# RWKV-7 scan: b and k transposed by VectorE blocks and ScalarE copies in place of TensorE

## The reference, cut to what matters

```python
def _rwkv7_scan(r, decay, k, v, kk, a, reverse):
    def step(S, inp):
        r_t, w_t, k_t, v_t, kk_t, a_t = inp
        sa = jnp.einsum('bhij,bhj->bhi', S, -kk_t)
        S = (S * w_t[:, :, None, :] + sa[..., None] * (kk_t * a_t)[:, :, None, :]
             + v_t[..., None] * k_t[:, :, None, :])
        y = jnp.einsum('bhij,bhj->bhi', S, r_t)
        return S, y
```

## Time and profile before

| | |
|---|---|
| median of 3 runs | 3921.93 us (3916.46 to 3925.49) |
| the profiled execution: its own time | 3919.46 us |
| its span, first to last instruction | 3917.7 us |
| mean granted TensorE clock | 0.964 of full |
| TensorE matmul busy, whole program | 3565.0 us, 91% |
| VectorE busy | 1859.1 us, 47% |
| ScalarE busy | 908.8 us, 23% |
| GpSimd busy | 179.5 us, 5% |
| the scan phase | from about 1660 to 2131 us of the span |

### The profile page before, as it was taken

How to read it: one execution, slowest core, us unless ns; L and a number is a source line. 1 busy time by engine, 2 the same in 40 slices (tenths; PEclk the granted TensorE clock), 3 DMA queues, 4 the chain that set the end, 5 groups by cost and what they waited for, 6 DMA issues and landing times. The chain is left out here.

```text
span 3917.7 us, 68126 instructions
## 1 busy us (share of the span) xinstructions
PE 3565.0 (91%) x28504; PEld 3035.6 (77%) x28504; DVE 1859.1 (47%) x2745; ACT 908.8 (23%) x1332; POOL 179.5 (5%) x336
## 2 busy tenths in 40 slices
PE   6999999999799991989998899777969999999997
PEld 5888888887677880989987677667858888888885
DVE  4544544544566206756655343303164544544546
ACT  2111111110433214433333622213031111111112
POOL 0000000000000000522221000000000000000000
PEclk9999999999899995999999999889989999999999
DMA  3010010010236312033333330110010110100101
GB/s 114 32 48 32 32 48 32 32 37 11 95 92 155 122 67 85 1 116 86 85 84 117 105 132 16 33 44 22 22 43 33 43 37 32 46 34 32 48 6 54
DMA packets 86028, 225.75 MB, mean 58 GB/s; under 512 B 6736, under 2 KB 53456, under 8 KB 79824
## 3 DMA queue, kind: packets, MB, share of 16 engines
q1 hardware_dynamic: 81808, 210.91, 16.9%
q10 hardware_dynamic: 4032, 12.06, 0.8%
HBM read 176.07 MB, written 46.87 MB: 57 GB/s over the span
## 5 line engine op out<-in xcount | busy, mean ns | idle before, releaser
L298 DVE TENSOR_TENSOR main_acc<-main_acc,ffn_psum 128x512 f32<-128x512 f32 (+1 forms) x1056 | 617.3, 598 | 853.8 <-PE ffn_psum L221 853.1
L210 PE MATMUL ffn_psum<-x_xh,ffn_wi_h 128*128 128x512 f32 (+1 forms) x2112 | 525.5, 357 | 49.3 <-DVE ffn_wi_l L287 49.3
L210 PE MATMUL ffn_psum<-x_xl,ffn_wi_h 128*128 128x512 f32 (+1 forms) x2112 | 525.3, 357 | 0.0
L210 PE MATMUL ffn_psum<-x_xh,ffn_wi_l 128*128 128x512 f32 (+1 forms) x2112 | 525.1, 357 | 0.0
L210 PEld LDWEIGHTS ffn_psum<-x_xh,ffn_wi_h 128*128 128x128 f32 x2112 | 372.8, 188 | 117.4 <-DVE ffn_wi_l L287 49.7
L210 PEld LDWEIGHTS ffn_psum<-x_xl,ffn_wi_h 128*128 128x128 f32 x2112 | 349.6, 188 | 61.3
L210 PEld LDWEIGHTS ffn_psum<-x_xh,ffn_wi_l 128*128 128x128 f32 x2112 | 349.9, 188 | 60.6
L221 PE MATMUL ffn_psum<-ffn_hid_h,ffn_wo_h 128*128 128x512 f32 (+1 forms) x1056 | 380.5, 360 | 12.5 <-DVE ffn_hid_l L306 10.0
L221 PE MATMUL ffn_psum<-ffn_hid_h,ffn_wo_l 128*128 128x512 f32 (+1 forms) x1056 | 377.6, 358 | 0.0
L221 PE MATMUL ffn_psum<-ffn_hid_l,ffn_wo_h 128*128 128x512 f32 (+1 forms) x1056 | 376.6, 357 | 0.0
L262 ACT CAST ffn_hid_h<-ffn_hid 128x1280 fp32r<-128x1280 f32 x44 | 55.6, 1265 | 1090.5 <-DVE ffn_hid L304 1090.5
(11 more groups left out here) (297 smaller groups left out, 5409.1 us busy)
## 6 DMA issues: line engine op xcount, KB each, us to landing
ffn_w_raw_in<-ffn_w_in_dram SPq DMA_DIRECT2D x44, 1024.0 KB, 7.0
rws_pack<-pack SPq DMA_DIRECT2D x160, 225.0 KB, 2.6
ffn_w_raw_out<-ffn_w_out_dram SPq DMA_DIRECT2D x44, 512.0 KB, 3.7
mixin_w_raw<-mix_w_in_dram SPq DMA_DIRECT2D x27, 512.0 KB, 3.7
pack<-mixin_pack SPq DMA_DIRECT2D x4, 2580.0 KB, 16.0
fin_raw<-ca_w_kv_dram SPq DMA_DIRECT2D x16, 512.0 KB, 3.7
pack<-mixin_pack SPq DMA_DIRECT2D x4, 1920.0 KB, 12.6
proj<-mixin_low ACTq DMA_DIRECT2D x12, 640.0 KB, 3.0
```

Of the source, the lines that this page charges most:

```text
L210: mm = nc.tensor.matmul(ps[:, at + c * BANK:at + c * BANK + tn], w[:, slot, cols], x[:, k, t0:t0 + tn], start=(k == 0 and j == 0), stop=(k ...
L298: nc.vector.tensor_tensor(acc[:, o, t0:t0 + tn], acc[:, o, t0:t0 + tn], ps[:, at:at + tn], ALU.add).then_inc(added, 1)
```

## The change

Five edits, all in `rwkv_scan_phase`:

1. `turn` leaves TensorE. b and k share a tile `bk` of 512 columns per direction, VectorE transposes it in 32x32 blocks to `bk_t` with one instruction per direction, and ScalarE's `rows_out` puts the four blocks of a head in place with four copies of 32 partitions by 256 elements, for each of two heads and two directions: sixteen small copies from SBUF in place of two of 128 by 512 from PSUM. Those copies stand between the levels on ScalarE.
2. `score_k` waits for `made` and `kr_set`, no longer for `rows_set`; `state` waits for `rows_set`.
3. `answer` is cut in halves of two q each, one between each two of levels 0 to 4; in `answer`, `state` and `right_side` the two heads alternate at each matmul.
4. `right_side(m, 0)` goes behind level 4, `right_side(m, 1)` behind the flips; ScalarE's `right_sides` behind its level 5 copies.
5. `turn_v` goes behind the last level; VectorE's `add_out` goes to the end of the step.

```diff
-        ar, b, k = per_slot("ar", TWO), per_dir("b", ONE), per_dir("k", ONE)
+        ar, bk, bk_t = per_slot("ar", TWO), per_dir("bk", [P, 2, 4, C]), per_dir("bk_t", [P, 2, 4, C])
+        b, k = [x[:, 0] for x in bk], [x[:, 1] for x in bk]
...
-            def turn(m, d):
-                pe.wait_ge(made[d], 4 * m + 2)
-                if m:
-                    pe.wait_ge(kr_set[d], m)
-                for j, src in enumerate((b[d], k[d])):
-                    for q in QS:
-                        for s in HEADS:
-                            mm = nc.tensor.matmul(halves(KB[d])[own(s), j, q], src[own(s), q], stack_ident[own(s)], start=True, stop=True)
-                mm.then_inc(turned[d], 1)
...
             def score_k(m):
                 for d in DIRS:
-                    pe.wait_ge(rows_set[d], m + 1)
+                    pe.wait_ge(made[d], 4 * m + 4)
+                    if m:
+                        pe.wait_ge(kr_set[d], m)
...
                     pe.wait_ge(u_set[d], n + 1)
+                    pe.wait_ge(rows_set[d], 8 * (n + 1))
...
             pe.wait_ge(consts_in, 16)
-            turn(0, 0)
-            turn(0, 1)
             turn_v(0)
...
+                for level in range(4):
+                    if more:
+                        raise_level(m, level)
+                    if n >= 0:
+                        answer(n, level // 2, level % 2)
                 if more:
-                    raise_level(m, 2)
+                    raise_level(m, 4)
                     right_side(m, 0)
-                    raise_level(m, 3)
-                    right_side(m, 1)
-                    raise_level(m, 4)
-                    if m + 1 < N:
-                        turn(m + 1, 0)
                     flip(m, 0)
                     flip(m, 1)
-                    if m + 1 < N:
-                        turn(m + 1, 1)
-                        turn_v(m + 1)
+                    right_side(m, 1)
                     last_level(m, 0)
                     last_level(m, 1)
+                    if m + 1 < N:
+                        turn_v(m + 1)
...
-            def rows_out(m, d):
+            def rows_out(m, d, s):
+
                 act.wait_ge(turned[d], m + 1)
                 if m >= 2:
                     act.wait_ge(h_done, m - 1)
-                nc.scalar.copy(rows[d][m % 2][:], halves(KB[d])).then_inc(rows_set[d], 1)
+                for i in range(2):
+                    for j in range(2):
+                        nc.scalar.copy(rows[d][m % 2][quadrant(s, j), :, :, part(i)], bk_t[d][quadrant(s, i), :, :, part(j)]).then_inc(rows_set[d], 1)
...
                     raised_out(m, 2)
+                    rows_out(m, 0, 0)
+                    rows_out(m, 0, 1)
                     raised_out(m, 3)
+                    rows_out(m, 1, 0)
                     raised_out(m, 4)
+                    rows_out(m, 1, 1)
+                    raised_out(m, 5)
                     right_sides(m)
-                    raised_out(m, 5)
+                    inverse_out(m)
                     if m + 1 < N:
-                        rows_out(m + 1, 0)
-                        rows_out(m + 1, 1)
                         v_out(m + 1)
-                    inverse_out(m)
...
+            def turn(m, d):
+
+                dve.wait_ge(made[d], 4 * m + 2)
+                if m:
+                    dve.wait_ge(rows_set[d], 8 * m)
+                nc.vector.transpose(bk_t[d][:].rearrange("p j q t -> p (j q t)"), bk[d][:].rearrange("p j q t -> p (j q t)")).then_inc(turned[d], 1)
...
-                if n >= 0:
-                    add_out(n)
                 if more:
                     for d in DIRS:
                         lower(m, 4, d)
+                    if m + 1 < N:
+                        turn(m + 1, 0)
+                        turn(m + 1, 1)
                     flipped_out(m)
+                if n >= 0:
+                    add_out(n)
```

More of the change, by code:

```diff
@@ L1371, in make @@
                         pool.wait_ge(scored_k[d], m)
-                    nc.gpsimd.tensor_tensor(b[d][:], pack[d][slot][:, :, B_COL:B_COL + C], grown[d][slot][:, :, now(d)], ALU.mult).then_inc(made[d], 1)
-                    nc.gpsimd.tensor_tensor(k[d][:], pack[d][slot][:, :, K_COL:K_COL + C], grown[d][slot][:, :, now(d)], ALU.mult).then_inc(made[d], 1)
+                    nc.gpsimd.tensor_tensor(b[d], pack[d][slot][:, :, B_COL:B_COL + C], grown[d][slot][:, :, now(d)], ALU.mult).then_inc(made[d], 1)
+                    nc.gpsimd.tensor_tensor(k[d], pack[d][slot][:, :, K_COL:K_COL + C], grown[d][slot][:, :, now(d)], ALU.mult).then_inc(made[d], 1)
                 for d in DIRS:
@@ L1472, in right_side @@
                     for s in HEADS:
-                        o = left(ST[d])[own(s), q]
-                        nc.tensor.matmul(o, kr[d][m % 2][own(s), q, 0], v_rows[own(s), chunk_of(m)[d], q], start=True, stop=False)
-                        mm = nc.tensor.matmul(o, ar[d][m % 2][own(s), q, 0], h[m % 2][own(s), d, q], start=False, stop=True)
+                        nc.tensor.matmul(left(ST[d])[own(s), q], kr[d][m % 2][own(s), q, 0], v_rows[own(s), chunk_of(m)[d], q], start=True, stop=False)
+                    for s in HEADS:
+                        mm = nc.tensor.matmul(left(ST[d])[own(s), q], ar[d][m % 2][own(s), q, 0], h[m % 2][own(s), d, q], start=False, stop=True)
                 mm.then_inc(rhs_done[d], 1)
@@ L1497, in state, with answer @@
                 mm.then_inc(h_done, 1)
[L1499 to L1506, removed]
-                    for s in HEADS:
[L1508 to L1512, removed]
+            def answer(n, d, half):
+                if half == 0:
+                    if n + 1 < N:
+                        pe.wait_ge(v_set, v_count(n + 1))
+                    if n:
+                        pe.wait_ge(y_added, 2 * n)
+                    pe.wait_ge(br_set[d], n + 1)
+                    pe.wait_ge(kr_set[d], n + 1)
+                for q in (2 * half, 2 * half + 1):
+                    for s in HEADS:
+                        nc.tensor.matmul(halves(YB)[own(s), d, q], h[n % 2][own(s), d, q], ar[d][n % 2][own(s), q, 1], start=True, stop=False)
+                    for s in HEADS:
+                        nc.tensor.matmul(halves(YB)[own(s), d, q], u[d][own(s), q], br[d][n % 2][own(s), q, 1], start=False, stop=False)
+                    for s in HEADS:
+                        mm = nc.tensor.matmul(halves(YB)[own(s), d, q], v_rows[own(s), chunk_of(n)[d], q], kr[d][n % 2][own(s), q, 1], start=False, stop=True)
+                if half:
+                    mm.then_inc(y_done[d], 1)
             pe.wait_ge(consts_in, 16)
-            turn(0, 0)
-            turn(0, 1)
             turn_v(0)
@@ L1599, in _ @@
             exponentials(1)
-            rows_out(0, 0)
-            rows_out(0, 1)
             v_out(0)
@@ L1693, in _ @@
             dve.wait_ge(consts_in, 16)
+            turn(0, 0)
+            turn(0, 1)
             for n in range(-1, N):
```

8 lines of the change are left out of this document (1 added, 7 removed).

## The result

| | before | after |
|---|---|---|
| median | 3921.77 us (3916.46 to 3925.49, 8 runs) | 3930.28 us (3927.47 to 3933.45, 8 runs) |
| profiled execution: its time, its span | 3919.46, 3917.7 us | 3928.19, 3926.4 us |
| ScalarE busy, whole program | 908.8 us | 1011.7 us |
| VectorE busy, whole program | 1859.1 us | 1888.4 us |

The ratio is 1.0024, with a 95% interval of 1.0013 to 1.0035: slower by 8.5 us, where 5.6 us faster was forecast. The time lies inside the stated range of 3904 to 3932 us and the change is clear of the noise, but its sign is the other one.

The account below looks back on a forecast made before the run. The prediction took SyncE's serial chain of packed loads, hidden under a busy TensorE, as the bound. An earlier start (-2.3) and faster loads (-3.3) gave -5.6 us, 3916.3 us against the median of 3921.93; range 3904 to 3932 us.

Parts of the forecast that it names:

- ScalarE's sixteen small copies: Between ScalarE's level copies: 0.32 us each, a step of 20.9 us, 21.4 with stalls, under the loads' 22.9; 0 on path.
- the rival, to which only 0.13 was given: ScalarE's copies between levels become the bound from about 0.41 us each; at 0.45, +15 us, 3931 us; chance 0.13.
- TensorE's clock: Waits at levels 2 and 3 drop TensorE's clock, losing 1.7 us each step: +10 us, 3926 us; chance 0.07.
- TensorE loses `turn`: 64 matmul records a step leave TensorE, 1.87 us a step, 35 us in 19 steps; direct value 0.
- with stalls of some 0.5 a step: Allowance for stalls in the scan's compute step, taking it from 20.9 to 21.4 us, below the loads' 22.9.
- The first load of chunk 2 comes earlier: SyncE's load goes out at about 1676.35 instead of 1678.63, moving the chain of loads up: -2.3 us.
- The loads themselves: SyncE's packed loads land sooner with fewer instruction fetches, 9 fewer from TensorE and one more from ScalarE: -3.3 us.
- VectorE's turns: Block transposes after level 4's masks, 0.71 us each, 1.4 a step; 0 on the path.
- Answers in halves and heads in turn: On TensorE, halves fill waits between levels and alternating heads may win something, all off the path: 0.
- The signs of being wrong: SyncE waiting for `made` or `v_turned`, VectorE ending last, copies over 0.4 us apart, or scan clock below 0.95.
- the second rival: TensorE was the bound after all, or loads speed up more: -12.4 us, 3909.5, or -9 us, 3913; chance 0.16.

Follow-up runs that it names:

- rows_early: Changed kernel with all sixteen small ScalarE copies moved from between the levels to the front of the step: 3902.13 us, ratio 0.9963 to the kernel before.
- vector_turns_twice: Changed kernel with each of VectorE's two transposes a step done twice, first into an unread buffer: 3931.08 us, ratio 1.0038 to the kernel before.
- heads_paired: Changed kernel with the two heads in state, right_side and answer ordered as before, not alternating: 3934.62 us, ratio 1.0053 to the kernel before.

## Why the prediction was wrong, step by step

- **"ScalarE's sixteen small copies": the step that failed.** They were put at 0.32 us from start to start, by two activations of 128 partitions; they start 0.425 apart. The prediction had each 0.1 us more at 1.2 to 1.6 us a step: 0.105 gives 1.3 to 1.7, so 20.9 becomes 22.2 to 22.6. Measured in such a step, without new v and without a fall of the clock: 22.34 in four of six, 22.65 at most, and 22.57 as the mean of all ten without a fall. The term on the path was put at 0; what the copies cost is shown by `rows_early`, where the same copies in another place let VectorE end 28 us earlier. Mechanism and place were right in the rival, to which only 0.13 was given. Its point at which the copies decide (0.41 us) rested on the loads as a floor at 22.6 us a step, which no run confirms. The Trainium skill's estimate beside it ("VectorE: DVE Perf Modes", The TRN2 errata) was 0.40 us a copy, and the copies are 0.40 long. Its step of 22.6 is close to 22.57 partly by luck, since it has the copies 0.40 apart and they are 0.425.
- **"TensorE's clock", chance 0.07:** came too, in nine steps of 19, at 0.53 us each by the means of steps and 0.41 among steps with new v, so some 4 to 5 us. The rival was given little because each wait would be under half of the one in the earlier trace rows. The wait ahead of level 3 was put at some 1.3 us and was 2.13: it stands behind eight of the mis-sized copies, and 8 x 0.105 is 0.84.
- **The sum at VectorE's end:** 19 x 0.43 us for steps without a fall = 8.2; 9 x 0.53 for the falls, less the 3.0 us of the one before, 1.8; the first u 1.0 earlier: +9.0. Measured +8.7. This adds up measured steps and so is an account, not a test. One step holds 4.1 of the 9.8 us by which the 19 grew together: the last took 19.65 us before and 23.70 after. It prepares no next chunk, so it had no `turn` to lose, and it got the sixteen copies all the same.
- **"TensorE loses `turn`": 0, since the chain of loads ends the phase.** The loads did end last, by 2.0 us, and still weren't the bound: with two in flight the time stayed, with half of `turn` gone it fell by 16 us. The 22.9 us a chunk were read as a floor; they fell with TensorE's work. In the changed kernel TensorE's 1.87 us were lost to the copies and the clock.
- **The stretch "with stalls of some 0.5 a step":** taken upon one short step of 21.25 us. The mean before was 22.30, so steps with new v and the rest cost 1.0 and not 0.5.
- **"The first load of chunk 2 comes earlier": -2.3, right.** In the execution after, the scan's first load goes out 1.72 us earlier (1662.75 for 1664.47), and the first of chunk 2 4.10 us earlier (1674.53 for 1678.63), so the change moved it by 2.4. It won nothing, because the loads no longer end the phase.
- **"The loads themselves": -3.3, too small, and without value.** 78 large fetches instead of 92 (9 fewer and 1 more were expected), and the 144 landings add up to 392.2 us instead of 409.1: -17. How much of that the fetches are isn't shown.
- **VectorE's turns:** put at 0.71 us, 0.67 to 0.71 measured, and 0 on the path, as the trace of `vector_turns_twice` shows. Answers in halves and heads in turn: 0 and at most a gain, also right.
- **The signs of being wrong:** three of the four came (SyncE's waits for v, VectorE last, copies over 0.4 apart); the clock stayed above 0.95. ScalarE's waits for packs were to rise to 20 us or more and fell to 4.9, in two waits, from 14.2. The step was to be about 22.7 us, set by the loads, and is 22.82, set by the copies: the number is right by luck.
- **A slip:** the second rival's -12.4 does not follow from its terms, 9 x 1.1 + 2.3 = 12.2. Nothing hangs on it.

## What to carry to other kernels

Work that leaves the busiest engine pays only if it doesn't land in another engine's queue ahead of something that the first waits for: look for the receiving engine's idle stretch before the cost of the instructions, since between the levels the same sixteen copies let the scan end 28 us later than in ScalarE's idle stretch of the same step. Price an instruction by its own form, and where only a neighbour's row is at hand, let a sum that turns within its bounds carry the chance. That a chain ends last by 2 us does not make it the bound, when a second one runs beside it at the same pace: take each away in turn.

## What the runs showed of the hardware

- A ScalarE copy of 32 partitions by 256 elements from SBUF takes 0.40 us and starts 0.425 us after the one before; activations of 128 by 260 from SBUF take 0.41 and start 0.32 apart. The small ones don't overlap.
- The granted clock fell to 0.50 for 3.4 us at a time after single waits of 2.1 us of TensorE, but not after each: in nine steps of 19 in the changed kernel, and in all 19 with a second wait of 1.1 to 1.9 us. It fell after shorter ones too: in `rows_early` once after idle times of 0.94 and 0.40 us (the stretches before and after it began to fall):

```profile
1736.30:1739.70 3.40, 2.05 (x75) 1.77 (x74) 1.00 (x4) 1.24 (x4) 0.00 (x0) 1.00 0.24 73
1739.70:1743.10 3.40, 3.40 (x50) 3.40 (x47) 1.11 (x3) 3.21 (x9) 0.00 (x0) 0.50 0.34 92
```

- One load at a time, a load's landing differs with what runs beside it, in one trace each: a mean of 2.84 us before, 2.72 after, 2.73 with half of `turn` gone, and 2.62 in `heads_paired`, for which no run shows the reason. With two in flight it is 3.23 us each, and the packed loads of the kernel before end 33 us sooner.
